# Short convolution's projections by seven half-size products per weight tile

## The reference, cut to what matters

```python
def short_conv_mixer(h, w_in, conv_w, w_out):     # h: 256 x 2048, w_in: 2048 x 8192, w_out: 2048 x 2048
    p = h @ w_in
    bg, cg, hv, g = jnp.split(p, 4, axis=-1)
    y = bg * dw_conv(cg * hv, conv_w)             # three taps along the tokens
    return (jax.nn.silu(g) * y) @ w_out
# around it: h = modulate(rms_norm(x, norm_g), shift, scale); x = x + gate * mixer(h); then rms_norm_2 and the third block
```

## Time and profile before

| | |
|---|---|
| median of 3 runs | 2940.47 us (2939.39 to 2945.11) |
| profiled execution | 2939.39 us |
| its span, first to last instruction | 2936.8 us |
| TensorE busy | 2876.0 us, 98% |
| TensorE weight loads busy | 2203.2 us, 75% |
| VectorE busy | 797.4 us, 27% |
| ScalarE busy | 396.5 us, 14% |
| mean granted TensorE clock | 0.993 |

### The profile page before, as it was taken

The page is one execution under the profiler, slowest core; times in us unless marked ns, Lnnn a source line. Parts: engine busy times, 40 slices in busy tenths (PEclk is TensorE's granted clock), DMA queues, the critical chain, the costliest instruction groups (busy, mean ns, idle before and its releaser), DMA issues. The chain is left out here.

```text
span 2936.8 us, 30098 instructions
## 1 busy us (share of the span) xinstructions
PE 2876.0 (98%) x12144; PEld 2203.2 (75%) x12144; DVE 797.4 (27%) x1530; ACT 396.5 (14%) x777; POOL 51.4 (2%) x72
## 2 busy tenths in 40 slices
PE   6999999999999999999999999999999999999999
PEld 1476776677666666666678888888888888888888
DVE  3733433333332255555550010100110100001010
ACT  0311111111110122222220010000000011111110
POOL 0000000000000000000000000000000000000000
PEclk9999999999999999999999999999999999999999
DMA  9765654565451333333325454555554454454441
GB/s 389 279 234 173 196 186 148 177 200 177 150 179 61 101 101 101 100 100 100 103 98 185 131 172 143 154 160 144 151 163 143 143 144 121 137 145 128 141 134 67
DMA packets 379149, 444.85 MB, mean 151 GB/s; under 512 B 20308, under 2 KB 351560, under 8 KB 378312
## 3 DMA queue, kind: packets, MB, share of 16 engines
q1 hardware_dynamic: 351088, 352.76, 39.4%
q0 software_dynamic: 19520, 75.50, 7.4%
q10 hardware_dynamic: 8472, 15.58, 1.4%
HBM read 439.56 MB, written 4.26 MB: 151 GB/s over the span
## 5 line engine op out<-in xcount | busy, mean ns | idle before, releaser
L464 PE MATMUL bank<-hT,w 128*128 128x256 f32 (+1 forms) x6144 | 1625.0, 425 | 6.1 <-ACT hT L1027 4.6
L464 PEld LDWEIGHTS bank<-hT,w 128*128 128x128 f32 x6144 | 1168.6, 191 | 424.1 <-issue 297.5
L464 PE MATMUL bank<-w,hT 128*128 128x256 f32 (+1 forms) x2176 | 461.7, 373 | 0.0
L464 PEld LDWEIGHTS bank<-w,hT 128*128 128x128 f32 x2176 | 403.0, 190 | 59.8 <-issue 8.1
L464 PE MATMUL bank<-yT,w 128*128 128x256 f32 x2048 | 445.1, 379 | 1.5 <-DVE yT L1728 1.0
L464 PEld LDWEIGHTS bank<-yT,w 128*128 128x128 f32 x2048 | 388.2, 190 | 54.4 <-DVE yT L1728 1.2
L1027 ACT ACTIVATE work<-bank 128x512 f32<-128x512 f32 (+3 forms) x292 | 153.6, 555 | 1649.3 <-PE bank L464 1644.3
L1559 DVE SCALAR_TENSOR_TENSOR work<-xT,silc,work 128x512 f32<-128x512 f32 x240 | 180.5, 752 | 40.6 <-DMA xT<-in_ada_w 32.6
L1027 ACT ACTIVATE work<-work 128x512 f32<-128x512 f32 (+4 forms) x243 | 135.5, 558 | 214.4 <-DVE work L1625 149.4
L464 PE MATMUL bank<-work 128*128 128x256 f32 (+2 forms) x400 | 117.0, 413 | 6.2 <-DVE work L1530 2.6
L464 PEld LDWEIGHTS bank<-work 128*128 128x128 f32 x400 | 74.6, 196 | 27.5 <-issue 12.0
(11 more groups left out here) (113 smaller groups left out, 841.4 us busy)
## 6 DMA issues: line engine op xcount, KB each, us to landing
w<-in_na_ssd_w_in SPq DMA_DIRECT2D x48, 2048.0 KB, 8.4
xT<-in_ada_w POOLq DMA_DIRECT2D x64, 1024.0 KB, 5.6
w<-in_sc_w_in SPq DMA_DIRECT2D x32, 2048.0 KB, 10.5
w<-in_w_in SPq DMA_DIRECT2D x32, 2048.0 KB, 10.6
w<-in_na_ssd_w_out SPq DMA_DIRECT2D x16, 2048.0 KB, 8.4
w<-in_ada_w SPq DMA_DIRECT2D x12, 2048.0 KB, 12.1
w<-in_na_ssd_w_in SPq DMA_DIRECT2D x16, 1024.0 KB, 7.5
w<-in_sc_w_out SPq DMA_DIRECT2D x8, 2048.0 KB, 8.2
```

Source lines behind the costliest of these rows:

```text
L464: return nc.tensor.matmul(dst, lhsT, rhs, start=start, stop=stop, skip_group_check=free)
```

## The change: what it does, and the diff

Each weight tile is seen as a 2 by 2 arrangement of quarters (1024 rows by 128 columns) and the tokens as a 2 by 2 arrangement too (1024 features by 128 tokens). Strassen's scheme in Winograd's form gives the tile's four output quarters from seven products of quarters in place of eight. A product is 8 matmuls of a 128x128 weight block against 128 token columns, so a tile is 56 matmuls of 128 columns where it was 32 of 256.

- Weight sums: VectorE makes four differences of quarters per tile, each 128 partitions by 1024 elements; three go to a buffer (`sums_x` or `sums_y`), one overwrites a quarter of the slot.
- Token sums: four per projection, made once for "sc" (1024 elements each) and in two parts for "sco" (768, then 256).
- The seven products of a tile go into two banks; a second pair of banks (3 and 4) alternates with 0 and 1.
- ScalarE copies both banks (512 and 384 columns) to `staged`; VectorE joins them in six additions (`combine`) to the tile's output.
- In "sc", VectorE makes the weight sums of the tile after next behind each `combine`; in the last iteration (i = 7) it also makes the weight sums of the second tile of "sco" and the first part of the token sums ahead of the silu and the last two chunks of `yT`.
- Apart from that, in `chband` the sum of squares of q is issued a projection earlier, and its Ln and Exp with it.

```diff
-              ("sc", 8, 4, [1, 2, 3, 4]), ("sco", 2, 4, [1, 2, 3, 4]), ("sb", 4, 4, [1, 2, 3, 4]),
+              ("sc", 8, 8, [2, 4, 6, 8]), ("sco", 2, 8, [2, 4, 6, 8]), ("sb", 4, 4, [1, 2, 3, 4]),
...
+        SEVEN = [bank[0], bank[1], bank[3], bank[4]]
+        def product(dst, weights, tokens, ready=None):
+            for kc in range(EIGHT):
+                if ready:
+                    pe.wait_ge(ready[0], ready[1] + kc + 1)
+                last = mm(dst, weights[:, kc, :], tokens[:, kc, :], kc == 0, kc == EIGHT - 1)
+            return last
+        def seven(phase, s, i, x, sums, rows=None, made=None):
+            loaded(s, phase, i)
+            pair = (SEVEN[2 * s % 4], SEVEN[(2 * s + 1) % 4])
+            for n in range(2):
+                g = 2 * s + n
+                pe.wait_ge(acc_free, BANKS[phase] + i * PHASE[phase][2] + g - (1 if phase == "sc" and is_first(i) and g < 2 else 3))
...
+            product(a(0), quarter(s, 0, 0), x(0, 0), rows)
+            product(a(1), quarter(s, 1, 0), x(0, 1), rows and (rows[0], rows[1] + EIGHT))
+            pe.wait_ge(t_made, TILES[phase] + 4 * i + s + 1)
+            if made is None:
+                product(a(3), quarter(s, 0, 1), sums[3])
+                product(a(2), t[:, 1, :, :], sums[2]).then_inc(acc_full, 1)
+                product(b(0), t[:, 0, :, :], sums[1])
+                product(b(1), quarter(s, 1, 1), sums[4])
+                product(b(2), t[:, 2, :, :], x(1, 1)).then_inc(acc_full, 1)
+            else:
+                product(b(2), t[:, 2, :, :], x(1, 1))
+                pe.wait_ge(s_made, made + 1)
+                product(a(3), quarter(s, 0, 1), sums[3])
...
         def sc(i):
             for s in range(SLOTS):
-                loaded(s, "sc", i)
-                dst = accumulate("sc", s, i)
-                for ch in range(2):
-                    last = featured(dst[:, ch * T:(ch + 1) * T], s, ch, T,
-                                    (lambda kc: 2 * DC + kc + 1) if is_first(i) and s + ch == 0 else None)
-                last.then_inc(acc_full, 1)
+                if is_first(i) and s == 0:
+                    seven("sc", s, i, H, H_SUM, (norm_out, 2 * DC), 0)
+                else:
+                    seven("sc", s, i, H, H_SUM)
...
+                if i + s == 0:
+                    seven("sco", s, i, Y, Y_SUM, (sc_y, 0), 8)
...
+        def ch_sums(i, n, sq):
+            pe.wait_ge(acc_free, BANKS["ch"] + 4 * i + 1 + n)
+            wait(pe, ch_lnfree, 2 * i + n)
+            mm(bank[2][:, :], ONES, sq.rearrange("p a b -> p (a b)")).then_inc(ch_ss, 1)
...
             project2("ch", 1, i, first)
+            ch_sums(i, 0, q2sq)
...
-            for n, sq in enumerate((q2sq, k2sq)):
-                pe.wait_ge(acc_free, BANKS["ch"] + 4 * i + 1 + n)
-                wait(pe, ch_lnfree, 2 * i + n)
-                mm(bank[2][:, :], ONES, sq.rearrange("p a b -> p (a b)")).then_inc(ch_ss, 1)
+            ch_sums(i, 1, k2sq)
...
+        def squares_of_sco():
+            for t in range(9):
+                if t < 8:
+                    staging("sco", t // 4, t % 4)
+                if t > 0:
+                    act.wait_ge(x_new, t)
+                    square(t - 1)
+        def staging(phase, i, s):
+            banks = (bank[0], bank[1]) if s % 2 == 0 else (bank[3], bank[4])
+            flat = staged.rearrange("p a b -> p (a b)")
+            act.wait_ge(acc_full, BANKS[phase] + i * PHASE[phase][2] + 2 * s + 1)
+            wait(act, c_made, TILES[phase] + 4 * i + s)
+            A(flat[:, 0:4 * P], banks[0][:, :], ACT.Copy).then_inc(acc_free, 1)
+            act.wait_ge(acc_full, BANKS[phase] + i * PHASE[phase][2] + 2 * s + 2)
+            A(flat[:, 4 * P:7 * P], banks[1][:, 0:3 * P], ACT.Copy).then_inc(acc_free, 1)
...
+        def weight_sums(phase, i, s, link):
+            dve.wait_ge(w_loaded[s], loads(s, phase, i))
+            t = sums_of(s)
+            link(v.tensor_tensor(t[:, 0, :, :], quarter(s, 0, 1), quarter(s, 0, 0), ALU.subtract))
+            v.tensor_tensor(quarter(s, 0, 1), quarter(s, 1, 1), quarter(s, 0, 1), ALU.subtract)
+            link(v.tensor_tensor(t[:, 1, :, :], quarter(s, 1, 1), t[:, 0, :, :], ALU.subtract))
+            v.tensor_tensor(t[:, 2, :, :], quarter(s, 1, 0), t[:, 1, :, :], ALU.subtract).then_inc(t_made, 1)
...
+        def combine(phase, i, s, dst, link):
+            dve.wait_ge(acc_free, BANKS[phase] + i * PHASE[phase][2] + 2 * s + 2)
+            c = lambda ch, a: dst[:, ch, a * P:(a + 1) * P]
+            p = lambda n: staged[:, n, :]
+            v.tensor_tensor(partial[:, 0, :], p(0), p(2), ALU.add)
+            link(v.tensor_tensor(c(0, 0), p(0), p(1), ALU.add))
+            link(v.tensor_tensor(partial[:, 1, :], partial[:, 0, :], p(3), ALU.add))
+            v.tensor_tensor(dst[:, 1, :].rearrange("p (a b) -> p a b", a=2), partial,
+                            p(4).unsqueeze(1).broadcast_to([P, 2, P]), ALU.add)
+            link(v.tensor_tensor(c(0, 1), partial[:, 1, :], p(6), ALU.add))
+            v.tensor_tensor(c(1, 0), c(1, 0), p(5), ALU.add).then_inc(c_made, 1)
+            dve.wait_ge(c_made, TILES[phase] + 4 * i + s + 1)
...
+                    if ahead and b == 1:       # add_out of the phase before, last iteration
+                        ahead(0)
+                        ahead(1)
...
+        def add_short(squares):
+            for t in range(8):
+                combine("sco", t // 4, t % 4, u_b, link)
...
+                last.then_inc(x_new, 1)
+                if t < 6:
+                    weight_sums("sco", (t + 2) // 4, (t + 2) % 4, link)
+                if t >= 2:
+                    link(add_squares(t - 1, squares))
             add_squares(7, squares).then_inc(norm_sum, 1)
...
+        dve.wait_ge(norm_out, 3 * DC)
+        token_sums(H, H_SUM, (0, EIGHT), link)
         def sc(i, link):
-            dve.wait_ge(acc_free, BANKS["sc"] + 4 * i + 3)
+            combine("sc", i, 0, u_b, link)
+            weight_sums("sc", i, 2, link)
+            combine("sc", i, 1, u_c, link)
+            weight_sums("sc", i, 3, link)
+            combine("sc", i, 2, u_h, link)
+            weight_sums("sc", i + 1, 0, link)
             link(v.tensor_tensor(u_pad[:, :, 1:T + 1], u_c, u_h, ALU.mult))
...
             link(v.tensor_tensor(u_out, u_out, u_b, ALU.mult))
+            combine("sc", i, 3, u_g, link)
+            weight_sums("sc", i + 1, 1, link)
+            if isinstance(i, int) and i == 7:
+                token_sums(Y, Y_SUM, (0, 6), link)
             dve.wait_ge(sc_e, i + 1)
             link(silu(u_e, u_g, u_e))
             for ch in range(2):
                 v.tensor_tensor(chunk(yT, 2 * i + ch), u_out[:, ch, :], u_e[:, ch, :], ALU.mult).then_inc(sc_y, 1)
...
+        dve.wait_ge(sc_y, 16)
+        token_sums(Y, Y_SUM, (6, EIGHT), link)
+        add_short(10)
```

More of the change, by code:

```diff
@@ L235, in program @@
     u_out = L(2, T)
+    sums_y = L(3, 8, P)
+    staged, partial = L(7, P), L(2, P)
+    L.at = WORK - 3 * 8 * P
+    sums_x = L(3, 8, P)
+    assert u_pad.shape and 7812 <= WORK - 3 * 8 * P
     L = Lay(work, WORK)
@@ L274, in program, with halves, quarter, sums_of @@
     PHASE = {ph[0]: ph for ph in PHASES}
+    TILES = {"sc": 0, "sco": 32}
+    EIGHT = 8
+    def halves(t, first, a, k):
+        return t[:, first + EIGHT * k:first + EIGHT * (k + 1), a * P:(a + 1) * P]
+    def quarter(s, k, n):
+        return w[s][:, EIGHT * k:EIGHT * (k + 1), n * P:(n + 1) * P]
+    H = lambda a, k: halves(hT, 0, a, k)
+    H_SUM = {j: hT[:, EIGHT * (n // 2):EIGHT * (n // 2 + 1), T + (n % 2) * P:T + (n % 2 + 1) * P]
+             for n, j in enumerate((1, 2, 3, 4))}
+    Y = lambda a, k: halves(yT, 0, a, k)
+    Y_SUM = {j: halves(yT, DC, n % 2, n // 2) for n, j in enumerate((1, 2, 3, 4))}
+    def sums_of(s):
+        return sums_x if s % 2 == 0 else sums_y
+    def loads(s, phase, i):
+        g = GROUPS[phase]
+        extra = 0
+        if s == 1:
+            extra = 16 * (i + 1) if phase == "ssd" else (16 * 8 if g > GROUPS["ssd"] else 0)
+        if s == 3 and g > GROUPS["ssd"]:
+            extra = -16 * 8
+        if s == 3:
+            extra -= 16 * EARLY
+        return 16 * (g + 1) + 16 * i + extra
     acc_full, acc_free = sem("acc_full"), sem("acc_free")
@@ L469, in loaded @@
         def loaded(s, phase, i):
[L470 to L478, removed]
+            pe.wait_ge(w_loaded[s], loads(s, phase, i))
         def accumulate(phase, n, i):
@@ L846, in out_short @@
+        iterations(pe, 8, sc)
+        for i in range(2):
+            for s in range(SLOTS):
+                if i + s == 0:
+                    seven("sco", s, i, Y, Y_SUM, (sc_y, 0), 8)
+                else:
+                    seven("sco", s, i, Y, Y_SUM)
         def out_short(phase, n):
@@ L1257, in _, with square, squares_of_out @@
         ssd_rms(7)
[L1260 to L1272, removed]
+        def square(t):
+            if t == 0:
```

(37 more changed lines are left out.)

38 lines of the change are left out of this document (30 added, 8 removed).

## The result

The changed kernel takes 2900.72 us (median of 4, 2899.64 to 2904.33) against 2942.62 us of the kernel before, run beside it (median of 4): ratio 0.986, interval 0.9843 to 0.9877. The forecast was 2900 us. In another session it gave 2899.47 against 2940.2 us, ratio 0.9862 (0.9847 to 0.9877).

A forecast was written before the change was run, and what follows sets the result against it. TensorE, busy for 98% of the span, was taken as the only bound. The terms sum to -40.7 us from the profiled 2939.4, 2898.7; that execution lies 1.1 us under the median, so 2900 us, range 2886 to 2930.

The forecast's parts named there:

- 40 tiles: Both projections: 112 records of 111.7 ns make a tile 12.51 us instead of 13.81, -52.0 us over all tiles.
- start of "sc": First "sc" tile, partly at half clock: token sums arrive without a stall, tile 15.0 us instead of 16.7, -0.4 us further.
- idle time at "sco", with the last chunk, and the clock there: Start of "sco": TensorE waits behind VectorE's sums for the last chunks, +10.0 us, and half clock afterwards, +2.9 us.
- end of "sco": Behind the last "sco" tile: copy and joining stand bare ahead of the additions before the norm, +2.9 us.
- chband: Last block's band attention: TensorE's four waits for ScalarE's Ln go, a projection now lying between, -4.1 us.
- The pace of the stream: Both projections: 128-column matmuls with fresh weights cost 111.7 ns a record, taken from short streams in the trace.
- Rival 1: Both projections: each tile's four semaphore waits leave weight loads bare, +30 us, 2930 us; chance 0.14.
- Rival 2: Both projections: weight loads and matmuls take turns, 220 ns a record, about 3380 us; chance 0.04.
- Rival 3: "sc": VectorE becomes the bound, costing above 50 us per iteration, whole gain gone at 55; 2980 us at 60; chance 0.06.

The follow-up runs named there:

- Experiment 2: Changed kernel with 64 or 96 token columns per product matmul, or 64 only in every third of four "sc" tiles: 3347.76, 2899.16 and 2901.23 us.
- experiment 1: Kernel before, each 256-column matmul of both projections split into two of 128 columns, without sums: 2961.43 us against 2939.39, ratio 1.0076.
- experiment 3: Changed kernel with each tile's last weight sum made two or four more times: 2901.91 and 2932.25 us.
- Experiment 4: Changed kernel, last "sc" iteration: silu and last chunks ahead of next-tile weight sums, 2891.54 us; also one token sum and its product earlier, 2891.40 us.
- band_only: Kernel before with only the edit in the last block's band attention (first sum of squares a projection earlier): 2937.23 us against 2940.20, ratio 0.9989.
- extra4: Changed kernel with the last weight sum of every tile made five times, 5.0 us more VectorE work per tile: 2932.25 us.

## Why the prediction was right, point by point

| term | forecast | measured |
|---|---|---|
| 40 tiles | -52.0 | -52.3 (13.813 to 12.506 us) |
| start of "sc" | -0.4 | -0.1 |
| idle time at "sco", with the last chunk, and the clock there | +12.9 | +12.3 |
| end of "sco" | +2.9 | +2.7 |
| `chband` | -4.1 | -3.4 |
| sum | -40.7 | -40.8 |

The measured tile is (2155.21 - 1767.51)/31 between the 384-wide copies of the first and the last tile of "sc", and the same in "sco". The start of "sco" is 24.85 us from the copy of the last tile of "sc" to that of tile 0 of "sco" (2155.21 to 2180.06), less 12.51. Of these 12.3 us 9.25 are the idle time and some 2.9 the price of 5.9 us of work at half clock. The end is 4.87 in place of 2.50 us ahead of the norm's sum, and 3.58 in place of 3.26 from there to the third block. Held against the stretches, A fell by 37.3 and B by 3.3 us, 40.6 in all; the medians fell by 41.9 us in one session and 40.7 in the other. That the sum is met within 0.2 us is partly luck: four of the terms are off by 0.3 to 0.7 us and cancel, and the time ahead of "sc" alone varies by more. In the one pair of profiles the span fell by 37.7 us only, since its 2.96 us ahead of "sc" went the other way.

**The pace of the stream.** The step rested on three short streams, of 128, 8 and 4 records; it held over 400 us at 111.6 ns. Experiment 2 shows that the 112 of the 64-column stream was the right one to carry over: the columns do not enter. Rival 1 is refuted: four waits per tile cost nothing measurable. Rival 2 is refuted as well: experiment 1 has loads and matmuls of all 128 rows back to back at 111.6 ns, which taking turns could not give. The rule of the Trainium skill (TensorE: Matmul & The Clock Gate, The mechanism) that a load overlaps a matmul only in other row groups does not hold for this stream (the same section also lets a load into the background weight buffer go ahead of running matmuls); the measurement decides.

**VectorE.** The 1024-wide subtraction, which I had bounded at 1209 and 1225 ns, takes 1225. Joining and weight sums end 7.5 us after the tile's end (1974.95 less 1967.4), forecast 7.8. Its share in "sc" is 62% where I forecast 68: my 33.8 us per iteration held all its short waits, and 31.2 us are busy. Rival 3's point of decision lies where it was put (experiment 3).

**Start and end of "sco".** Right in mechanism and size: TensorE resumed at E + 12.5 (forecast 12.9), after 9.25 us of idle time (forecast 9.8). At the end the copy and joining cost +2.4 us, and the clock, which falls with the norm's sum and not 0.4 us behind its start as before (2272.4 for 2272.44, 2307.5 for 2307.11), +0.3. Experiment 4 shows that it was order, not amount, of VectorE's work.

**Start of "sc".** The token sums came in time; only the saving was mis-sized, by 0.3 us. The first 16 matmuls took 6.2 us (1752.16 to 1758.37, forecast 6.1). My 15.0 us for the tile ended with its last matmul, though, and the 16.7 us that I held it against ended with ScalarE's copy, 0.2 us later; from first matmul to copy it is 15.35.

**chband.** The term was right by luck in part: it is a gain of 5.1 us with 1.7 us given back. The four waits did go, 4.3 us. From the start of the third block to the 2.31 us wait that ends the band attention `band_only` is 5.1 us shorter (511.89 against 517.03 us), so each wait that went was worth some 0.2 us more than its idle time; my reading is that a record is 379 ns in the array and 215.7 ns from its neighbour, so behind the last record before a wait 0.16 us more go by. Behind that wait the granted clock is 0.50 for one spell of 3.4 us in every kernel with this edit, where the kernel before has 1.00. Windows just behind the wait, of `band_only` and then of the kernel before:

```profile
2829.00:2832.00 3.00, 3.00 (x9) 2.46 (x8) 0.56 (x1) 0.00 (x0) 0.00 (x0) 0.50 0.00 0
```
```profile
2828.00:2831.00 3.00, 3.00 (x15) 2.66 (x14) 0.54 (x1) 0.00 (x0) 0.00 (x0) 1.00 0.00 0
```

From the wait to the end `band_only` takes 111.1 us where the kernel before takes 109.4: the 1.7 us. That the edit causes this spell is likely, and not shown: nothing was run that sets it apart.

## What to carry to other kernels

Trading matmuls for vector work pays where TensorE is the only bound; count the trade in weight blocks, not in columns: here an eighth fewer products were worth 9.5% of a tile (1.31 of 13.81 us), because a record costs 111.6 ns with 128, 96 and 64 columns alike. Look for the price at the seams, not in the stream: the stream hid 26 us of added VectorE work per iteration (busy 5.3 us before, 31.2 now, and some 17 us are still idle), while 12.3 us were lost where the work of a later tile stood ahead of the two chunks that TensorE waited for. A long idle time on TensorE costs a spell at half clock besides (some 2.9 us for the one of 9.25), so closing it gives more than its own length. Length alone does not tell which idle times cost one: at the start of "sco" 0.74 and 2.80 us did not, inside "sc" of `extra4` two of the three of 1.9 us did.

## What the runs showed of the hardware that was not expected

With 64-column matmuls through both projections the granted clock stayed at 0.50 for 976 us (1753.4 to 2729.7), though TensorE was busy without a gap for hundreds of them (740 us of 740 in the window shown), and the kernel was 447 us slower with half the columns. With 96 columns, and with 64 in one tile of four, the clock came back to 1.00 within 5.1 us of the first matmul of "sc". Why it stays down with 64 is not shown. What sets the pace of the narrow records follows that clock: 213.2 ns at 0.50, 111.6 at 1.00.
